# Three layer borders rewritten: a signal of its own for the norm's reciprocal, feature values on VectorE, and low parts between the two operations of the norm

## The reference

```
# layers 0 and 1 (no norm ahead of h; a layer norm behind each)
h = x * (1 + scale) + shift
y = mixer(h @ w_in ...) @ w_out              # gMLP with pooling (0), latent attention (1)
x = layer_norm(ALPHA * x + (1 + gate) * y, ln_g, ln_b)

# layers 2 and 3 (a root mean square norm ahead of h)
h = rms_norm(x, norm_g) * (1 + scale) + shift
y = concat(retention(...) * silu(rg), stick_breaking(...) * silu(sg)) @ w_out
x = x + gate * y
out = rms_norm(x, final_g)                   # behind layer 3
```

## Time and profile before

| | |
|---|---|
| median of 3 runs | 1363.75 us (1362.11 to 1366.34) |
| the profiled execution's own time | 1364.07 us |
| its span | 1362.3 us |
| TensorE busy | 1327.5 us, 97% |
| VectorE busy | 913.3 us, 67% |
| ScalarE busy | 565.8 us, 42% |
| GpSimd busy | 301.4 us, 22% |
| mean granted clock of TensorE | 0.99 of full speed |

### The profile page before, as it was taken

The page is one execution under the profiler, slowest core; times in us unless marked ns, Lnnn a source line. Parts: engine busy times, 40 slices in busy tenths (PEclk is TensorE's granted clock), DMA queues, the critical chain, the costliest instruction groups (busy, mean ns, idle before and its releaser), DMA issues.

```text
span 1362.3 us, 17437 instructions
## 1 busy us (share of the span) xinstructions
PE 1327.5 (97%) x6781; PEld 1123.8 (82%) x6781; DVE 913.3 (67%) x1330; ACT 565.8 (42%) x854; POOL 301.4 (22%) x207
## 2 busy tenths in 40 slices
PE   6999999999999999999999999999999999999997
PEld 5998888778878878888888778888888888888885
DVE  6754544774485568988678787676776577676653
ACT  2423222221264246656422475543342566534430
POOL 0100200065420015555344100001115300011123
PEclk9999999999999999999999899999999999999998
DMA  9654443323424422213344243313324322211111
GB/s 379 185 167 139 139 139 140 138 94 139 147 96 137 140 66 62 70 36 93 93 139 140 93 139 115 115 50 140 112 74 141 137 93 69 87 63 62 62 63 62
DMA packets 31378, 155.14 MB, mean 114 GB/s; under 512 B 4160, under 2 KB 4288, under 8 KB 20032
## 3 DMA queue, kind: packets, MB, share of 16 engines
q1 hardware_dynamic: 31296, 154.03, 33.8%
HBM read 151.92 MB, written 2.10 MB: 113 GB/s over the span
## 4 chain that ended last, share of the span: by engine, by line
PE 83%; DVE 7%; issue 4%; ACT 2%; DMA 1%; POOL 1%; SPq 0%; DVEq 0%; ACTq 0%; POOLq 0%
PE bank L844 24%; PE bank L846 24%; PE bank L845 24%; PE bank L1320 1%; DVE acc L1699 1%; PE bank L1008 1%; PE bank L1152 1%; PE bank L1294 1%; PE bank L990 1%; DMA ada_first<-adat 1%; PE bank L1156 1%; DVE qn_lo L1965 1%; PE bank L1296 1%; PE bank L1139 1%; DMA w_raw<-wt 1%
## 5 line engine op out<-in xcount | busy, mean ns | idle before, releaser
L844 PE MATMUL bank<-h_lo,w_hi 128*128 128x512 f32 (+1 forms) x1014 | 399.1, 394 | 4.5 <-DVE h_lo L1842 1.8
L846 PE MATMUL bank<-h_hi,w_hi 128*128 128x512 f32 (+1 forms) x1014 | 393.8, 388 | 0.0
L845 PE MATMUL bank<-h_hi,w_lo 128*128 128x512 f32 (+1 forms) x1014 | 393.5, 388 | 0.0
L1658 DVE TENSOR_TENSOR w_lo<-w_raw,w_hi 128x2048 fp32r<-128x2048 f32 (+2 forms) x91 | 207.0, 2275 | 87.2 <-ACT w_hi L1365 87.2
L844 PEld LDWEIGHTS bank<-h_lo,w_hi 128*128 128x128 f32 x1014 | 190.6, 188 | 45.4 <-issue 5.8
L846 PEld LDWEIGHTS bank<-h_hi,w_hi 128*128 128x128 f32 x1014 | 190.4, 188 | 39.7
L845 PEld LDWEIGHTS bank<-h_hi,w_lo 128*128 128x128 f32 x1014 | 190.8, 188 | 37.9 <-issue 0.5
L1365 ACT ACTIVATE w_hi<-w_raw 128x2048 fp32r<-128x2048 f32 (+2 forms) x91 | 166.9, 1834 | 88.3 <-PE bank L846 77.8
L1447 ACT ACTIVATE tmp<-bank 128x512 f32<-128x512 f32 x48 | 28.6, 596 | 126.1 <-PE bank L846 116.7
L2269 POOL TENSOR_SCALAR q_dup<-rot_y 128x512 fp32r<-128x512 f32 x8 | 11.9, 1492 | 301.5 <-DVE rot_y L1710 301.5
L1699 DVE SCALAR_TENSOR_TENSOR acc<-ada_raw,cond_pair,acc 128x1024 f32<-128x1024 f32 x45 | 58.5, 1301 | 0.0
(11 more groups left out here) (357 smaller groups left out, 2679.7 us busy)
## 6 DMA issues: line engine op xcount, KB each, us to landing
w_raw<-wt SPq DMA_DIRECT2D x83, 1024.0 KB, 6.0
ada_raw<-adat SPq DMA_DIRECT2D x96, 256.0 KB, 3.9
ada_raw<-adat SPq DMA_DIRECT2D x32, 512.0 KB, 3.7
ada_first<-adat SPq DMA_DIRECT2D x16, 512.0 KB, 12.0
w_raw<-wt SPq DMA_DIRECT2D x8, 640.0 KB, 5.3
spare_raw<-wt SPq DMA_DIRECT2D x3, 1024.0 KB, 5.8
x<-xt SPq DMA_DIRECT2D x4, 512.0 KB, 15.6
out<-outf SPq DMA_DIRECT2D x8, 256.0 KB, 2.2
```

The costliest lines, as they stand in the source:

```text
L844: pe.matmul(dst, ah, bl, start=start, stop=False, skip_group_check=True)
L845: pe.matmul(dst, al, bh, start=False, stop=False, skip_group_check=True)
L846: return pe.matmul(dst, ah, bh, start=False, stop=stop, skip_group_check=True)
L1658: dve.tensor_tensor(w_lo[wb[T]][:, 0:n], w_raw[wb[T]][:, 0:n], f(w_hi[wb[T]][:, 0:n]), ALU.subtract).then_inc(w_lo_done, 1)
```

## The change

There are three edits.

1. VectorE raises a new semaphore `str_scale` behind the reciprocal at the two layer norms. TensorE waits for it ahead of the broadcast of `st_r`, and for `str_done` only ahead of that of `st_mr`.
2. At borders 1 and 3 the feature values are computed by VectorE (`h_value`) and no longer by GpSimd. Each one waits for the VectorE instruction that makes its input. Border 2 keeps them on GpSimd.
3. At border 2 the two operations of the norm are separate functions, `scaled` and `plain`, and `h_low(k)` stands between `scaled(k + 2)` and `plain(k + 2)`. The last two low parts are no longer behind both products into `tmp`: each follows its own.

```diff
@@ stat_bcast on TensorE
-                    pe.wait_ge(str_done, d["stat"] + 1)
                     for src, bk in zip((st_rho if d["lhs"] == "derived" else st_r, st_mr), d["banks"]):
+                        if len(d["banks"]) == 2 and src is st_r:
+                            pe.wait_ge(str_scale, STAT_SUMS[d["stat"]])
+                        else:
+                            pe.wait_ge(str_done, d["stat"] + 1)
@@ VectorE
+            def h_value(l, k, tok, t):
+
+                dve.tensor_scalar(tmp[:, 2 + k % 2, tok], t[:, tok], h_scale[:, l, k:k + 1], h_shift[:, l, k:k + 1],
+                                  ALU.mult, ALU.add).then_inc(h_v_half if tok is LEFT else h_v_done, 1)
+
@@ statistics
                 if d["mean"]:
-                    link(ins)
+                    ins.then_inc(str_scale, 1)
+                    dve.wait_ge(str_scale, STAT_SUMS[si])
                     ins = dve.tensor_tensor(st_mr[:], st_mean[:], st_r[:], ALU.mult)
@@ h (border 3)
+                    first = H_T_BASE["h", l]
                     for tok, signal in ((LEFT, h_t_half), (RIGHT, h_t)):
                         dve.tensor_tensor(tmp[:, 0, tok], x[:, 0, tok], bank[:, 6, tok], ALU.mult).then_inc(signal, 1)
+                        dve.wait_ge(signal, l if tok is LEFT else first + 1)
+                        h_value(l, 0, tok, tmp[:, 0, :])
...
                         if k >= 2:
                             h_low(l, k - 1)
+                        if k < DC:
+                            dve.wait_ge(h_t, first + k + 1)
+                            h_value(l, k, slice(0, S), tmp[:, k % 2, :])
@@ ln (border 1)
+                        dve.wait_ge(signal, 1)
+                        h_value(1, 0, tok, x[:, 0, :])
...
                             dve.tensor_tensor(x[:, k, :], x[:, k, :], bank[:, 5, :], ALU.subtract).then_inc(h_t, 1)
+                            dve.wait_ge(h_t, k + 1)
+                            h_value(1, k, slice(0, S), x[:, k, :])
@@ ln_h (border 2)
+                    def scaled(k):
+                        if k < DC:
+                            link(dve.tensor_tensor(x[:, k, :], x[:, k, :], bank[:, 6, :], ALU.mult))
+
                     def plain(k):
-                        link(dve.tensor_tensor(x[:, k, :], x[:, k, :], bank[:, 6, :], ALU.mult))
-                        if k == 0:
-                            dve.wait_ge(stb_done, rho)
-                        dve.tensor_tensor(x[:, k, :], x[:, k, :], bank[:, 5, :], ALU.subtract).then_inc(ln_t, 1)
+                        if k < DC:
+                            dve.tensor_tensor(x[:, k, :], x[:, k, :], bank[:, 5, :], ALU.subtract).then_inc(ln_t, 1)
...
-                            h_low(l, 0)
-                            plain(2)
-                            continue
-                        dve.tensor_tensor(tmp[:, k % 2, :], x[:, k, :], bank[:, 4, :], ALU.mult).then_inc(h_t, 1)
-                        if k + 2 < DC:
-                            plain(k + 2)
-                            h_low(l, k)
-                    h_low(l, DC - 2)
-                    h_low(l, DC - 1)
+                        else:
+                            dve.tensor_tensor(tmp[:, k % 2, :], x[:, k, :], bank[:, 4, :], ALU.mult).then_inc(h_t, 1)
+                        scaled(k + 2)
+                        h_low(l, k)
+                        plain(k + 2)
@@ GpSimd
-                elif op in ("h", "ln", "ln_h"):
+                elif op == "ln_h":
```

More of the change, by code:

```diff
@@ L542, in build @@
         str_done = sem("str_done")
+        str_scale = sem("str_scale")
         stb_done = sem("stb_done")
@@ L2082, in _ @@
                             dve.tensor_tensor(x[:, k, :], x[:, k, :], bank[:, 5, :], ALU.subtract).then_inc(h_t, 1)
+                            dve.wait_ge(h_t, k + 1)
+                            h_value(1, k, slice(0, S), x[:, k, :])
                 elif op == "ln_h":
                     l, rho = d["l"], d["s"]
+                    def scaled(k):
+                        if k < DC:
+                            link(dve.tensor_tensor(x[:, k, :], x[:, k, :], bank[:, 6, :], ALU.mult))
                     def plain(k):
-                        link(dve.tensor_tensor(x[:, k, :], x[:, k, :], bank[:, 6, :], ALU.mult))
-                        if k == 0:
-                            dve.wait_ge(stb_done, rho)
-                        dve.tensor_tensor(x[:, k, :], x[:, k, :], bank[:, 5, :], ALU.subtract).then_inc(ln_t, 1)
+                        if k < DC:
+                            dve.tensor_tensor(x[:, k, :], x[:, k, :], bank[:, 5, :], ALU.subtract).then_inc(ln_t, 1)
                     dve.wait_ge(stb_scale, 2)
+                    scaled(0)
+                    dve.wait_ge(stb_done, rho)
                     plain(0)
                     derived_root(rho)
+                    scaled(1)
                     plain(1)
```

## The result

The changed kernel takes 1367.25 us (median of 8 runs, 1364.96 to 1368.13), the kernel before on the same chip 1363.35 us (8 runs, 1361.69 to 1366.34). The ratio is 1.0021, 95% interval 1.0012 to 1.0031: 2.9 us by the ratio, 3.9 us by the two medians. The profiled execution took 1367.09 us itself, with a span of 1365.3 us, against 1364.07 and 1362.3 before: +3.0 both times, at a mean granted clock of 0.990 in both.

The account below looks back on a forecast made before the run. TensorE, busy 97% of the span, was taken as the bound, so only its waits at the borders count. Border 2 +2.4, border 1 +0.4, border 3 +0.2 sum to +3.0 us: 1366.7 us on the median 1363.75, range 1362.2 to 1369.6.

Parts of the forecast that it names:

- chunk 1 of border 2 earlier: Border 2: scaled(2) fills VectorE's idle 0.71 us, so TensorE takes chunk 1 at 770.73 in place of 771.66, 0.93 us won.
- round of border 2: Border 2: each chunk's round grows from 2.52 to about 2.90 us, above TensorE's 2.73, so TensorE waits 0.17 us each.
- chunk 6, given back: Border 2: chunk 6 starts at 785.23 against 785.40 before, so the 0.93 us are nearly given back.
- chunk 7 later for TensorE, start: Border 2: the round trip stands open twice, so TensorE starts chunk 7 at 787.53 against 786.08 before.
- the same with the restart: Border 2: chunk 7's delay plus 0.11 us for the slower matmul behind a wait, +1.56 us on TensorE.
- scores later, VectorE's row: Behind border 2: VectorE's work without a pause moves by the last low part's whole delay, so the scores come +2.4 us later.
- border 1: Border 1: feature values in VectorE's row, partly offset by edit 1, cost +0.4 us; bounds −0.3 and +0.7.
- border 3: Border 3: two values ahead of the first low part cost +0.2 us, the rest hidden beneath TensorE; bounds 0 and +0.4.
- value of 512 and 256 columns: Borders 1 and 3: one feature value on VectorE takes 0.54 us for 512 columns and 0.41 for 256.
- The gain stays: Rival: border 2's round stays under 2.73 us and chunk 7 is on time, border 2 −0.93, total 1362.7 us; chance 0.25.
- TensorE's clock falls: Rival: waits of about 1.5 us at border 1 and border 2's chunk 7 cost 1.7 us each, 1370.1 us; chance 0.09.
- The delay is absorbed behind border 2: Rival: VectorE's queue has slack, only TensorE's 1.56 us counts, 1365.9 us; chance 0.66 together with the forecast.

Follow-up runs that it names:

- e3: Edit 3 alone (the new order at border 2) against the kernel before: 1366.36 us, ratio 1.0022.
- e7: Edit 3 with one VectorE accumulation moved from ahead of the low parts of q to behind those of k, against the kernel before: 1365.94 us, ratio 1.0019.
- second profile: The changed kernel, unaltered, profiled and timed again against the kernel before: 1367.47 us, ratio 1.0035.
- e6: Edit 1, and edit 3 only for chunk 0's low part at border 2, against the kernel before: 1363.66 us, ratio 0.9997.
- e2: Edit 2 alone (feature values on VectorE at borders 1 and 3) against the kernel before: 1364.08 us, ratio 1.0000.
- e4: Edit 3 with the last two low parts put back behind both products into tmp, against the kernel before: 1366.60 us, ratio 1.0020.

## Why the prediction was right, step by step

The forecast was 1366.7 us and the time 1367.25; the sum was +3.0 us against the profiled execution, and that is what its span and own time show (+3.0). That these two agree to the tenth is in part luck, since single executions of one kernel differ by more. What is shown is the mechanism, and its largest term, border 2, by size too.

| step | predicted | profile after | what tells it |
|---|---|---|---|
| chunk 1 of border 2 earlier | 0.93 | 0.91 | segment; e3 the same |
| round of border 2 | 2.90 us | 2.93 | low parts 769.25, 772.18 |
| chunk 6, given back | −0.17 | −0.02 | 784.62; 785.40 before |
| chunk 7 later for TensorE, start | +1.45 | +1.57 | 1.30 of wait |
| the same with the restart | +1.56 | +1.70 | 787.70; 786.76 before |
| scores later, VectorE's row | +2.4 | +2.53 | e3 +2.52, e7 +1.52 |
| border 1 | +0.4 | +0.5 | second profile, same clock; by the means +0.8 |
| border 3 | +0.2 | not shown | +0.12 in one pair |
| value of 512 and 256 columns | 0.54, 0.41 us | 0.55, 0.41 | L1837 |

**Border 2.** Both halves held: the idle 0.71 us was filled and 0.91 us won, and then one instruction no longer covered the round trip of 1.69 us over ScalarE and GpSimd, as two had. The size of +2.4 was 0.13 short, since a round takes 2.93 and not 2.90. It was ScalarE's way that ended last in each round (0.45 <-ACT h_hi), GpSimd's only at chunk 7: `plain`, gain and bias, rounding. The working put 0.03 us between the end of the rounding and the low part, and the trace has 0.09 (771.29 + 0.80 to 772.18). VectorE's row was indeed without slack: taking 1.28 us out of it (e7) gave back 1.0.

**Border 1.** The working on VectorE's grid holds: counted from `st_r`, the second profile of the changed kernel has the first subtraction at 2.30 us, the low part of chunk 1 at 7.61 and TensorE at 8.36, where the working had 2.29, 7.60 and 8.34. Edit 1's 0.22 us are in it. The values outweigh them, because the first low part now has two of them ahead of it. Chunk 7's first product came 0.37 later where 0.29 was summed (394.86 against 394.57), and the restart took 0.16 in place of 0.11: together 0.5 in place of 0.4. What the working didn't see is that its base scatters: the kernel before was read at 8.25 us for chunk 1, and the six other profiles of kernels with the old values have 7.96 to 8.29. By the means border 1 costs 0.8, at the upper bound of +0.7 or a little over it.

**Border 3.** The 0.12 us stands in one pair of profiles. Kernels with the old border 3 have 26.90 to 27.84 us from `st_r` to the scores, those with the new one 27.07, 27.12 and 28.67. The term of +0.2 is neither shown nor refuted.

**The rivals.** *The gain stays* fell: chunk 7 was not on time, and the rounds were 2.93 us. It needed what e6 has. *TensorE's clock falls* was not seen where it was placed. In both profiles of the changed kernel it is 1.00 from 775 to 800 us, so it is no part of the loss that they show. At border 1 the long wait ahead of the first product did come, 1.58 us in the second profile and 1.76 in e2's, and behind it the clock was 1.00 from 376 to 384 us in both. The 0.50 from 370 to 376 us in the first profile lies ahead of that product, and e6_first_only_signal, with the old values, has 0.52 there. But e4 shows it behind the scores, at a price of 1.6 us where the rival had 1.7: the mechanism exists, a few microseconds later than placed, and it came in one of the five profiles of kernels with a late chunk 7. *The delay is absorbed behind border 2* fell with e7: without its edit the row of VectorE decides.

**What is left over.** With border 1 as in the pair of equal clock, the segments sum to +3.1 to +3.2 us, by the means of border 1 to +3.4 or so. The medians differ by 3.9 in the first comparison and 3.5 in the second, and at equal clock the changed kernel lies 3.7 us above the kernel before (both sets of its runs, ±0.6). At equal clock edits 1 to 3 alone sum to +3.9, near the whole, though edits 1 and 2 alone (+0.5 each, ±0.6) are not clear of nothing. Where the remaining 0.3 us or so would be lost is open: it is within the intervals, and no experiment was aimed at it.

**The values.** The rule weighed in the prediction, from the Trainium skill, "VectorE: DVE Perf Modes", section "The perf-mode tier table (the rule you actually need)", with the fixed part from its errata section, would have made them 0.42 and 0.29 us by estimate. The traces show 0.55 and 0.41, so the measurement decides against it here. It is the fixed part that is larger: 256 columns more cost 0.14 us, about half of what they cost in the subtraction of the low part (0.43 to 0.69). Border 1 came out as a loss and not as the −0.3 of that rule.

## What to carry to other kernels

Before an instruction is pulled out from between a value's production and its use, count the round trip over the other engines (here 1.69 us by the forecast, 1.73 in the trace) and what is left to cover it (1.92 us of starts before, 1.2 after). As long as it is covered, the loop's period is the sum of the starts (1.92 + 0.60 = 2.52 us). Once it isn't, the period is the round trip plus everything that now stands outside it (1.73 + 1.20 = 2.93), and only a comparison with the consumer's period (2.73 us) says whether that is paid. Peel the iteration in which the engine idles, and leave the loop as it is (e6). And where a late iteration is followed by a row of work without a pause on the same engine, the whole delay of that engine counts, not only the consumer's wait: look which work in the row can go behind the part that the consumer needs (e7). Both are shown by the segments, and by the times only at equal clock and barely.

And before a difference of 0.1 to 0.5 us between two profiles is believed, look at the same segment in every profile whose code is the same there. At border 2 it repeats within 0.02 us, at border 1 within 0.4, at border 3 only within 1.

## What the runs showed of the hardware that I had not expected

- The granted clock at the borders differs between executions of one and the same kernel. From 360 to 400 us the changed kernel lost 3.6 us of full speed in its first profile (0.91) and 1.6 in its second (0.96). The runs of the kernel before scatter over nearly 6 us (1361.16 to 1367.09 in 35 runs), which is more than the change moves, and they go with the mean granted clock, −0.66 us for each 0.001. Segments of the timeline that lie where the clock is 1.00 repeat within 0.02 us between profiles of kernels that have the same code there (7.65, 7.65, 7.66; 6.74, 6.75, 6.75).
- Waits of TensorE of 1.30, 0.87 and 0.87 us between 785 and 795 us left its clock at 1.00 in both profiles of the changed kernel and in e3's, and shorter ones (0.49, 0.86, 0.87) were followed by the lower level in e4's. The sum of the waits alone doesn't decide it; what does, these runs don't show.
- GpSimd's value of 128x512 took 0.77 us, and 1.26 beside a VectorE instruction with two inputs from SBUF. Serial work on the two engines is thus not simply the sum of what each takes alone: in e4 half a microsecond of the repair went there, and the right half's value at border 1 takes 0.80 to 0.82 in place of 0.56 in the profiles of all kernels that have it on GpSimd.
